# A fused transformer trunk on one core: raw and split weight slots in a new order, one VectorE split and one scaled row moved, unread TensorE products at two seams

## What is computed

```python
logits = t @ w_router
top_v, top_i = lax.top_k(logits, 2)
gate = one_hot(top_i, 8) weighted by softmax(top_v)
gu   = einsum('nd,edf->nef', t, w_gu)
act  = silu(gu[..., :3584]) * gu[..., 3584:] * gate[..., None]
out  = einsum('nef,efd->nd', act, w_down)
```

## Time and profile before

| | before |
|---|---|
| median of 3 runs | 1340.87 us (1340.11 to 1343.79) |
| profiled execution, its own time | 1341.47 us |
| its span (first to last instruction) | 1339.7 us |
| TensorE busy | 1305.5 us (97%) |
| VectorE busy | 760.3 us (57%) |
| ScalarE busy | 642.8 us (48%) |
| mean granted TensorE clock | 0.995 |
| DMA | 431.64 MB, mean 322 GB/s |
| chain that ended last, by engine | PE 90%, DVE 5%, ACT 2%, DMA 2% |

### The profile page before, as it was taken

The page is one execution under the profiler, slowest core; times in us unless marked ns, Lnnn a source line. Parts: engine busy times, 40 slices in busy tenths (PEclk is TensorE's granted clock), DMA queues, the critical chain, the costliest instruction groups (busy, mean ns, idle before and its releaser), DMA issues.

```text
span 1339.7 us, 18721 instructions
## 1 busy us (share of the span) xinstructions
PE 1305.5 (97%) x7498; PEld 980.5 (73%) x7498; DVE 760.3 (57%) x900; ACT 642.8 (48%) x775; POOL 50.4 (4%) x128
## 2 busy tenths in 40 slices
PE   7999999999999989999999999999999999999997
PEld 7987888887987667777776767776667777666762
DVE  6855655544748659863386643467635367655332
ACT  5645644433557746743365633355542356534221
POOL 3000000000103400000000000000000000000000
PEclk9999999999999989999999999999999999999999
DMA  9452555555462248999999999999999999999996
GB/s 361 160 187 94 204 189 177 188 185 188 154 221 75 87 173 303 340 391 427 428 427 427 423 410 428 428 428 426 427 421 428 426 427 429 428 414 425 426 428 281
DMA packets 36084, 431.64 MB, mean 322 GB/s; under 512 B 4000, under 2 KB 4000, under 8 KB 5152
## 3 DMA queue, kind: packets, MB, share of 16 engines
q1 hardware_dynamic: 35856, 429.94, 79.4%
q10 hardware_dynamic: 144, 0.52, 0.1%
HBM read 429.40 MB, written 1.05 MB: 321 GB/s over the span
## 4 chain that ended last, share of the span: by engine, by line
PE 90%; DVE 5%; ACT 2%; DMA 2%; issue 1%; POOL 0%; POOLq 0%; SPq 0%; DVEq 0%; ACTq 0%
PE bank L1579 20%; PE bank L1580 20%; PE bank L1581 20%; PE bank L2137 14%; PE bank L2158 7%; DMA raw<-in_moe 1%; PE bank L2087 1%; PE bank L2184 1%; DVE w_lo L1484 1%; PE bank L1965 1%; PE bank L2195 1%; ACT w_hi L584 1%; PE bank L1950 1%; DMA raw<-in_wts 1%; DVE ht_lo L1020 1%
## 5 line engine op out<-in xcount | busy, mean ns | idle before, releaser
L1484 DVE TENSOR_TENSOR w_lo<-raw,w_hi 128x2048 fp32r<-128x2048 f32 x114 | 258.0, 2288 | 144.7 <-ACT w_hi L895 144.4
L1579 PE MATMUL bank<-w_hi,ht_hi 128*128 128x512 f32 (+1 forms) x768 | 304.1, 396 | 1.8 <-DVE ht_lo L1020 0.9
L1581 PE MATMUL bank<-w_hi,ht_lo 128*128 128x512 f32 (+1 forms) x768 | 296.4, 386 | 0.0
L895 ACT ACTIVATE w_hi<-raw 128x2048 fp32r<-128x2048 f32 x114 | 214.6, 1910 | 128.1 <-DMA raw<-in_moe 112.3
L996 DVE TENSOR_TENSOR w_lo<-raw,w_hi 128x2048 fp32r<-128x2048 f32 x70 | 159.8, 2291 | 115.5 <-ACT w_hi L584 115.4
L1580 PE MATMUL bank<-w_lo,ht_hi 128*128 128x512 f32 (+1 forms) x568 | 217.9, 384 | 0.0
L1579 PEld LDWEIGHTS bank<-w_hi,ht_hi 128*128 128x128 f32 x768 | 144.4, 188 | 49.6 <-issue 17.5
L584 ACT ACTIVATE w_hi<-raw 128x2048 fp32r<-128x2048 f32 x71 | 135.5, 1918 | 91.1 <-PE bank L1581 89.0
L1581 PEld LDWEIGHTS bank<-w_hi,ht_lo 128*128 128x128 f32 x768 | 144.3, 188 | 30.1
L1484 DVE TENSOR_TENSOR more_lo<-more,w_hi 128x2048 fp32r<-128x2048 f32 x50 | 114.1, 2290 | 81.8 <-ACT w_hi L895 81.7
L895 ACT ACTIVATE w_hi<-more 128x2048 fp32r<-128x2048 f32 x50 | 95.9, 1918 | 100.9 <-PE bank L1581 53.6
(11 more groups left out here) (334 smaller groups left out, 1481.7 us busy)
## 6 DMA issues: line engine op xcount, KB each, us to landing
raw<-in_moe SPq DMA_DIRECT2D x112, 2048.0 KB, 12.8
more<-in_moe SPq DMA_DIRECT2D x54, 2048.0 KB, 12.5
raw<-in_wts SPq DMA_DIRECT2D x71, 1024.0 KB, 4.8
more<-in_moe SPq DMA_DIRECT2D x4, 1024.0 KB, 14.9
xs<-in_x SPq DMA_DIRECT2D x2, 512.0 KB, 4.0
out<-xn SPq DMA_DIRECT2D x4, 256.0 KB, 2.0
pk<-in_packed SPq DMA_DIRECT2D x1, 517.0 KB, 7.9
g1b<-in_norm_ffn ACTq DMA_DIRECT2D x1, 512.0 KB, 3.7
```

What stands on the lines that cost most here:

```text
L895: a(w_hi[:, hi_order(n) % SPLIT, :], slot_raw(n), ACT.Copy).then_inc(s_hi, 1)
L1484: v.tensor_tensor(slot_lo(n), slot_raw(n), w_hi[:, hi_order(n) % SPLIT, :].bitcast(F32), ALU.subtract).then_inc(s_lo, 1)
L1579: mm(out_, sh, mh, start=first, stop=False)
L1581: return mm(out_, sl, mh, start=False, stop=last)
```

## The change

Four edits, made on all engines that they concern.

1. **Order of the (up 1, down 0) phases.** The first chunk is as before (four ups, two downs). Then come three groups of eight raw up slots and four split down slots, with `turned_b` after the first four ups and after the last four. The splits of ScalarE and VectorE in these phases stand behind `silu_b`, `turned_b` and `product_b` and no longer ahead of them. The other phases keep their order.
2. **VectorE's split of slot `N0 + 1`** moves from between the low halves of tile 0 and the third residual part to a later place, behind the one-hot tile and ahead of the job tables.
3. **`gained(1)`** moves from behind the expert ranking to ahead of it.
4. **Unread products.** TensorE multiplies the identity by itself into a bank that nobody reads: 20 times at the start as soon as the identity is there (a new semaphore `s_ident`), 6 times behind the first transposes, and at the K/V seam 7 times ahead of the transposes, 5 times between their two tiles and 2 times behind them.

```diff
+    def downs_before(s):
+        if s < 6:
+            return max(s - 4, 0)
+        group, at = divmod(s - 6, 12)
+        return 2 + 4 * group + max(at - 8, 0)
...
-    def up_slot(c, h, u, paired):
+    def up_slot(c, h, u, paired, up):
+        if paired and up == 1:
+            group, odd = divmod(c + 1, 2)
+            return (12 * group - 6 + 4 * odd if c else 0) + 2 * h + u
         return (6 if paired else 4) * c + 2 * h + u
...
+    def down_slot(d, paired, down):
+        if paired and down == 0:
+            group, at = divmod(d + 2, 4)
+            return 12 * group + 2 + at if d >= 2 else 4 + d
         return 6 * (d // 2) + 4 + d % 2 if paired else d
+
+    def downs_after(c, down):
+        if down == 1:
+            return (c,)
+        return () if c % 2 else (c - 1, c) if c else (0,)
...
+        g.memset(consts[:, 3:4], 0.0).then_inc(s_ident, 1)
...
# ScalarE and VectorE, phase loop
-                split(min(last + MOE_AHEAD, length + 1) if paired else last + AHEAD)
+                if up == 0:
+                    split(min(last + MOE_AHEAD, length + 1) if paired else last + AHEAD)
...
+                if up == 1:
+                    split(min(last + MOE_AHEAD, length + 1))
...
# VectorE, router stage
         tile_low(5, 0, 6, (1, 7, 6, 2))
-        split_to(N0 + 1)
         residual(2, OUT_BANKS, N0 - 1, (2,))
         gained(0)
...
         tile_low(5, 1, 6, (4, 5, 3, 0), (2, 3))
+        gained(1)
...
         v.tensor_scalar(rf[5], rf[3], 2.0, None, ALU.is_lt).then_inc(s_selm, 1)
-        gained(1)
...
+        split_to(N0 + 1)
         for part in range(3):
             job_tables(part)
...
# TensorE
+        def unread(bank, n):
+            for _ in range(n):
+                mm(bank[:, 0:P], ident[:], ident[:], start=True, stop=True)
+
+        pe.wait_ge(s_ident, 1)
+        unread(B[5], 20)
         pe.wait_ge(s_const, 1)
         transposed(0, 2, (0, 1, 2, 3))
+        unread(B[5], 6)
         pe.wait_ge(s_half0, 1)
...
-        transposed(3, 6)
+        unread(B[6], 7)
+        transposed(3, 6, between=5)
+        unread(B[6], 2)
...
-                    for d in (2 * c, 2 * c + 1):
-                        down_part(i, first + down_slot(d, paired), d, down)
+                    for d in [2 * b + j for b in downs_after(c, down) for j in range(2)]:
+                        down_part(i, first + down_slot(d, paired, down), d, down)
```

More of the change, by code:

```diff
@@ L190, in trunk @@
     s_pc = sem("pool_chain"); s_ac = sem("act_chain"); s_dc = sem("dve_chain")
[L191 removed]
+    s_const, s_ident = sem("constants_ready"), sem("identity_ready")
     s_wshi, s_wslo = sem("small_hi"), sem("small_lo")
@@ L426, in _, with phase_loads @@
         rounds = sp.value_load(tab[0:1, 0:1], min_val=PAIRS - 1, max_val=PAIRS_MAX - 1)
-        def phase_loads(i, first, up, down):
+        def phase_loads(i, first, up, down, kind):
             n = first
@@ L435, in phase_loads @@
                         n += 2
-                if up is None and c == DOWN_SLOTS // 2 - 1:
+                    for b in downs_after(c, kind):
+                        load_pair(n, job_pair(bass.ds(down, 1), UP_SLOTS + 2 * b), i)
+                        n += 2
+                    continue
+                if c == DOWN_SLOTS // 2 - 1:
                     load(n, job_slot(bass.ds(down, 1), UP_SLOTS + 2 * c), i)
@@ L448, in round_loads @@
             e_b = expert(i * 2 + 2)
-            phase_loads(i, N0 + UP_SLOTS, e_b, expert(i * 2 + 1))
-            phase_loads(i, N0 + UP_SLOTS + JOB_SLOTS, expert(i * 2 + 3), e_b)
+            phase_loads(i, N0 + UP_SLOTS, e_b, expert(i * 2 + 1), 0)
+            phase_loads(i, N0 + UP_SLOTS + JOB_SLOTS, expert(i * 2 + 3), e_b, 1)
         for i in range(PAIRS - 2):
@@ L456, in _ @@
         e_b = expert(rounds * 2 + 2)
-        phase_loads(rounds, N0 + UP_SLOTS, e_b, expert(rounds * 2 + 1))
-        phase_loads(rounds, N0 + UP_SLOTS + JOB_SLOTS, None, e_b)
+        phase_loads(rounds, N0 + UP_SLOTS, e_b, expert(rounds * 2 + 1), 0)
+        phase_loads(rounds, N0 + UP_SLOTS + JOB_SLOTS, None, e_b, 1)
         sp.wait_ge(s_used, rounds * (2 * JOB_SLOTS) + (N0 + UP_SLOTS + JOB_SLOTS))
@@ L1499, in product_b @@
             def product_b(c):
-                dve.wait_ge(s_used, i * (2 * JOB_SLOTS) + (first + up_slot(c, 1, 1, paired) + 1))
+                dve.wait_ge(s_used, i * (2 * JOB_SLOTS) + (first + up_slot(c, 1, 1, paired, up) + 1))
                 dve.wait_ge(s_bsilu, i * 7 + (c + 1))
@@ L1509, in phase @@
                     continue
-                last = up_slot(c, h, 1, paired)
-                split(min(last + MOE_AHEAD, length + 1) if paired else last + AHEAD)
+                last = up_slot(c, h, 1, paired, up)
+                if up == 0:
+                    split(min(last + MOE_AHEAD, length + 1) if paired else last + AHEAD)
                 if up == 0 and h == 0:
@@ L1584, in wait_slot, with transposed @@
             pe.wait_ge(s_lo, splits_before(n) + 1)
-        def transposed(p, xn_count, banks=(0, 1, 2, 3)):
+        def unread(bank, n):
+            for _ in range(n):
+                mm(bank[:, 0:P], ident[:], ident[:], start=True, stop=True)
+        def transposed(p, xn_count, banks=(0, 1, 2, 3), between=0):
             for t in range(NT):
+                if t:
+                    unread(B[5], between)
                 pe.wait_ge(s_xn, xn_count - NT + t + 1)
@@ L2214, in phase @@
                         for u in range(2):
-                            gu(i, first + up_slot(c, h, u, paired), 2 * h + u, B[h], up)
+                            gu(i, first + up_slot(c, h, u, paired, up), 2 * h + u, B[h], up)
                     if c and h == 0 and up == 0:
@@ L2245, in phase @@
                 for d in range(2):
-                    down_part(i, first + length + down_slot(d, False), d, 1, 0)
+                    down_part(i, first + length + down_slot(d, False, 1), d, 1, 0)
             elif following is not None:
```

7 lines of the change are left out of this document (3 added, 4 removed).

## The result

| | before | changed |
|---|---|---|
| median of 5 runs each | 1340.87 us (1340.11 to 1343.79) | 1353.72 us (1349.15 to 1354.01) |
| ratio, 95% interval | | 1.008 [1.0069, 1.0092] |
| profiled execution, its own time | 1341.47 us | 1353.24 us |
| its span | 1339.7 us | 1351.4 us |
| mean granted TensorE clock | 0.995 | 0.989 |

The account below looks back on a forecast made before the run. TensorE was taken as the limit, with the DMA close behind (207.47 against 205.5 us a round). Terms 1.4 (start) + 1.4 (seam) + 1.37 (router) + 0.45 (joints) = 4.6 us; forecast median 1336.4 us, range 1334.0 to 1339.2.

Parts of the forecast that it names:

- The new waits ... No wait, though with little left: Experts' groups of four split downs: splits would be ready before TensorE needs them, the first with a margin of 1.4 us.
- The sign that I had named: Experts' rounds one to three: a TensorE wait for `w_lo` at the first of four split downs would make the prediction wrong.
- The slower rival: Experts' phases: the first of four splits comes late, 2.3 us at nine groups, 1357 us; chance 0.06.
- The last three don't count, since there TensorE already waits for the DMA: Last of the four reordered phases: its three chunk merges were given no gain, leaving 9 x 0.05 us.
- The joints: Experts' reordered phases: fewer changes between raw, transposed and split work on TensorE save 0.05 us a merge, 0.45 in all.
- The start: Kernel start: 20 + 6 unread products bring the high clock to the first products' steps, saving 1.4 us.
- The K/V seam: K/V seam: 7 + 5 + 2 unread products fill TensorE's idle gaps and keep the clock up, saving 1.4 us.
- The router: Router stage: the moved split removes a 1.56 us TensorE wait, the moved `gained(1)` costs 0.19; 1.37 us saved.
- Everything before the experts moves their loads too, because a load starts when TensorE frees its buffer, so the DMA's stream moves with it.: Experts' loads: time won ahead of the experts was taken to shift the DMA's stream too, so those terms count in the sum.
- the better case: Router clock also stays up through the gather, 1334.4 us by its own line; the range took it as 1334.0.

Follow-up runs that it names:

- e6: The changed kernel with nine unread products ahead of the next phase's second up slot, in TensorE's 2.19 us wait: 1347.11 us, 1.0047 of the kernel before.
- e1: The changed kernel with the look-ahead repaired, so a raw-up phase's last half chunk splits to the whole phase end again: 1341.06 us, 0.9992 of the kernel before.
- e5: The kernel before, with splits in a raw-up phase's last half chunk going to slot 42 and no longer 43: 1352.92 us, ratio 1.0085.
- e7: e1 with the last raw-up phase in the old order and its splits in the old places: 1339.20 us, 0.9980 of the kernel before.
- e3: The changed kernel without the unread products and the router moves, so the new slot order alone: 1356.79 us, 1.0107 of the kernel before.
- e8: The kernel before with the two router moves alone: 1341.35 us, ratio 0.9995.
- e4: The kernel before with the unread products of the start and the K/V seam alone: 1340.35 us, ratio 0.9991.
- e2: The kernel before with the unread products and both router moves, slots in the old order: 1339.26 us, ratio 0.9979.
- e12: e9 with VectorE's first three job-table parts moved behind the gathered low halves and the split after them: 1337.30 us, 0.9953 of the kernel before.
- e9: e2 with 14 more unread products in TensorE's two waits of the router stage: 1337.05 us, 0.9963 of the kernel before.
- e10: e7 with 14 more unread products in the router stage: 1337.69 us, 0.9972 of the kernel before.
- e11: The changed kernel itself, run again: 1354.01 us, 1.0087 of the kernel before.

## Why the prediction was wrong, point by point

- **"The new waits ... No wait, though with little left": this step failed.** I worked through the four splits of the phase's last group of downs, and stopped there: the two slots behind it, the first of the next phase, are split in the same call and were not in the sum. The bound `min(last + MOE_AHEAD, length + 1)` was in the code that the change touches, `last` moved from 39 to 37 at the edge, and I didn't put the new number in. Cost: 7.5 us of waits in three rounds (e6 against e1), and 3.1 of clock behind them (changed kernel against e6). e5 shows it from the other side. The sign that I had named, a wait for `w_lo` at the first of four split downs in rounds one to three, did not come, since the late split was another. The same item took the first chunk to be as before, since its slots are; but its splits moved behind `silu_b`, which costs 0.46 in round one. From the forecast of 1336.4 to 1353.7 it is 17.3: 11.3 in the rounds (10.9 lost, 0.45 forecast as a gain), 4.7 in the last raw-up phase, 0.5 less won ahead of the experts than the 4.2 of the sum, and the rest between medians and profiled executions.
- **The slower rival** came near in size (1357) by luck, since it had the wrong place. It had nine groups at 2.3 us; there are three boundaries at 2.5 and the clock. In the groups of four splits in rounds one to three there was no wait: e1's rounds two and three have none at all, and its round one only the 0.46 of the first chunk. Its chance of 0.06 was too low, since a change that moves splits behind other instructions of ScalarE and VectorE has more than one place where a split can be late, and I had priced one.
- **"The last three don't count, since there TensorE already waits for the DMA": wrong as well.** The last phase is where the DMA's landing decides, and a run of four splits asks for a slot earlier than two did. That is 2.0 us by e1 against e7, 0.8 of wait and the rest of clock; in the changed kernel it was 1.95 of wait and a clock low for about twice as long.
- **The joints.** Forecast 0.15 a round. With the look-ahead repaired, rounds two and three are 0.10 shorter. Round one is 0.4 longer, by the wait in its first chunk. The step from `turned_b` to raw work was 659.57 to 659.94, 0.37 and not 0.31. By what the Trainium skill (TensorEngine Tiling (Array Packing), Key Properties) says of a change of the tiling mode the prediction had worked out 0 for this edit. The 0.10 a round that was measured is nearer to the 0.15.
- **The start.** Forecast 1.4, and the steps were 0.12 from the first product on. The 20 fillers took 6.49 us, as forecast (6.7); the transposes behind them ended at 9.95 (by the prediction's own 8.4 and 16 x 0.136 it would be 10.6, and not the 10 that it gives). But the products at the low clock that they replace vary in number by chance: e3, with no fillers, ran its first product at 12.17 and stepped by 0.12 at once, and e5 at 12.61 with steps of 0.21 to 18.50. These are 27 steps and took 5.89 us, which at 0.12 would be 3.24. So the gain is between nothing and 2.7 from one execution to the next. In this pair of traces the 16th product came 2.1 us sooner (13.73 and not 15.87), 0.7 of it because the first did (11.86 and not 12.54). By 87 us 0.6 was left in the changed kernel, since its clock fell near 46 us.
- **The K/V seam.** Forecast 1.4. ScalarE's step behind the seam (L742, now L766) starts at 374.11 and no longer at 376.10, 1.99 sooner. Ahead of the seam the changed kernel was 0.65 early (VectorE's residual, at 330.75 and no longer at 331.40). The difference is 1.3. The low clock was there in all four kernels without the fillers (before, e3, e5, e8) and in none of the ten with them.
- **The router.** Forecast 1.37; 1.76 between the two traces at the gather (3.77 less the 2.01 brought along), 1.4 between e4 and e2. TensorE's wait for the third part shrank from 1.56 to 0.38, not to nothing.
- **"Everything before the experts moves their loads too, because a load starts when TensorE frees its buffer, so the DMA's stream moves with it."** True in the rounds (e2's split of a pair starts with its landing at 798.71, before 803.19: 4.5 of 4.6), but not to the end of the stream, where e12's loads were issued 6.8 earlier and landed 5.0 earlier. This term was missing from the sum. With the old order my terms give 4.2, and e2 won 2.1 by its median: 1.2 went in the last phase, and the rest is most likely falls of the clock by chance, for the profiled execution (1337.92, clock 0.996) won 3.5, and those with a clock of 0.993 to 0.995 took 1338.6 to 1341.1.
- **Two small slips in the sums.** 1340.87 less 4.6 is 1336.3, and the better case is 1334.4, where the range begins at 1334.0. Neither bears on the outcome.

## What to carry to other kernels

When an order of slots is changed, put the new index into every bound that is computed from it, at the first and the last step of each loop, and follow each call to the end of what it does; here one slot less of look-ahead behind an instruction that waits for TensorE cost 11.3 us of 1341. A wait of 2.2 us on TensorE can cost 1.6 more by the clock behind it, so unread products in a wait that can't be removed can pay for themselves (e6). And where two limits lie close (207.47 us of TensorE for 205.5 of DMA in a round), time that is won ahead of them arrives only in part: look for the phase in which the other limit takes over.

## What was not expected of the hardware

- The clock fell to 0.50 at places where TensorE's own work was the same as in other executions: near 46 us in the changed kernel, e1, e5 and e9, not in before, e2, e3, e4, e6, e7, e8, e10, e11 and e12; near 121 us in e1, e3 and e4. In the first of these TensorE was busy all the time by the profile (6.00 of 6.00 us, clock 0.72), right behind products of four rows (L1772). Near 121 us e4 fell behind a stretch in which TensorE was busy for 1.10 of 3.00 us, and e2 did not behind one of 1.20. Behind equal waits of 2.19 us the clock fell twice in three in the changed kernel, and three times in e3. One fall costs about 1.6 us, which is more than an edit that is worth 1.4 us by its own rows.
- What the clock does before 15.87 us at the start is chance too: full rate from 12.17 (e3), 15.87 (before), 15.98 (e8) or 18.50 us (e5), in kernels whose start is the same. The Trainium skill (TensorE: Matmul & The Clock Gate, Part 1) says that the point of this switch moves from run to run. These traces agree for the rise at the start, with the four times just given; that the falls in the list above come from the same is not shown.
- Unread products held the clock at 1.00 wherever they filled a wait: the seam, the three boundaries (e6) and the router stage (e9, e10, e12).
